# The values product of a fused two-block kernel: one fp32 product becomes three products of split operands

## The reference, cut to what matters

```python
sc = jnp.einsum('bqhd,bkhd->bhqk', q[:, s:e], k[:, :kend]).astype(jnp.float32) * scale
sc = jnp.where(mask[None, None], sc, -jnp.inf)
p = jax.nn.softmax(sc, axis=-1)
p = p.reshape(p.shape[0], A_HEADS, 2, e - s, kend)
w = p[:, :, 0] - lam * p[:, :, 1]
outs.append(jnp.einsum('bhqk,bkhd->bqhd', w.astype(v.dtype), v[:, :kend]))
```

## Time and profile before

| | us |
|---|---|
| median of 3 runs | 2394.51 (2392.45 to 2395.05) |
| the profiled execution, its own time | 2390.51 |
| its span in the trace | 2388.8 |
| PE busy | 2295.3 (96%) |
| PE weight loads busy | 1996.2 (84%) |
| DVE busy | 1601.9 (67%) |
| ACT busy | 1130.2 (47%) |
| POOL busy | 96.9 (4%) |

### The profile page before, as it was taken

One profiled execution on the slowest core, in us unless ns is written; L12 is line 12 of the kernel. 1 busy time (PEld: TensorE's weight loads), 2 busy tenths in 40 slices (PEclk: granted clock), 3 DMA queues, 4 the chain that ended last, 5 costly groups with the idle time before them and its releaser, 6 DMA issues.

```text
span 2388.8 us, 34521 instructions
## 1 busy us (share of the span) xinstructions
PE 2295.3 (96%) x13343; PEld 1996.2 (84%) x13343; DVE 1601.9 (67%) x1973; ACT 1130.2 (47%) x1693; POOL 96.9 (4%) x182
## 2 busy tenths in 40 slices
PE   6789999999989999999999999999999999999897
PEld 5678888887788888888888889999999999778786
DVE  6777677677768865666656776667667646666654
ACT  3345444443365543555445554444444455545443
POOL 0000000111100000000000000000000000000000
PEclk8789999999999999999999999999999999999999
DMA  9999788788857755555555655444444545433352
GB/s 337 357 358 357 255 265 280 232 314 311 317 176 252 271 198 187 183 190 179 194 194 176 210 179 164 157 142 142 142 142 142 167 151 153 146 124 107 106 194 106
DMA packets 229910, 492.95 MB, mean 206 GB/s; under 512 B 9618, under 2 KB 12392, under 8 KB 226696
## 3 DMA queue, kind: packets, MB, share of 16 engines
q1 hardware_dynamic: 210384, 432.05, 53.3%
q0 software_dynamic: 14144, 50.93, 6.4%
q10 hardware_dynamic: 5256, 8.20, 1.0%
HBM read 488.49 MB, written 2.10 MB: 205 GB/s over the span
## 4 chain that ended last, share of the span: by engine, by line
PE 82%; DVE 8%; DMA 4%; issue 2%; ACT 2%; SPq 0%; DVEq 0%; POOL 0%; POOLq 0%; ACTq 0%
PE ps L1722 31%; PE ps L1740 21%; PE ps L1755 14%; PE ps L1757 7%; DMA ada<-in_ada_w 2%; PE ps L2199 2%; DVE wlo L1029 2%; DVE acc L1089 2%; DMA mods<-in_ada_w 1%; PE ps L2026 1%; DMA raw<-in_a_w_in 1%; PE ps L2169 1%; ACT whi L521 1%; DVE acc L1038 1%; PE ps L1866 1%
## 5 line engine op out<-in xcount | busy, mean ns | idle before, releaser
L1029 DVE TENSOR_TENSOR wlo<-raw,whi 128x1024 fp32r<-128x1024 f32 x720 | 872.3, 1222 | 511.1 <-ACT whi L521 509.5
L521 ACT ACTIVATE whi<-raw 128x1024 fp32r<-128x1024 f32 x720 | 755.9, 1057 | 835.2 <-PE ps L1722 406.2
L1755 PE MATMUL ps<-xt__58,whi 128*128 128x512 f32 x1408 | 498.1, 399 | 0.9 <-DVE h L1221 0.7
L1757 PE MATMUL ps<-xt__58,wlo 128*128 128x256 f32 x1408 | 395.3, 281 | 0.0
L1722 PE MATMUL ps<-whi,xt__58 128*128 128x512 f32 x1024 | 331.9, 401 | 11.3 <-DVE xt__58 L1141 11.3
L1740 PE MATMUL ps<-xmh__59,whi 128*128 128x272 f32 x1088 | 323.3, 297 | 3.8 <-DVE ks L1426 3.1
L1755 PEld LDWEIGHTS ps<-xt__58,whi 128*128 128x128 f32 x1408 | 264.5, 188 | 67.3 <-DVE h L1221 2.2
L1740 PE MATMUL ps<-xmh__59,wlo 128*128 128x272 f32 x1088 | 315.7, 290 | 0.0
L1740 PE MATMUL ps<-xml__60,whi 128*128 128x272 f32 x1088 | 313.8, 288 | 0.0
L1757 PEld LDWEIGHTS ps<-xt__58,wlo 128*128 128x128 f32 x1408 | 266.0, 189 | 0.1
L1722 PEld LDWEIGHTS ps<-whi,xt__58 128*128 128x128 f32 x1024 | 196.9, 192 | 53.2 <-DVE xt__58 L1141 8.3
(11 more groups left out here) (297 smaller groups left out, 3272.6 us busy)
## 6 DMA issues: line engine op xcount, KB each, us to landing
raw<-in_a_w_in SPq DMA_DIRECT2D x128, 1024.0 KB, 5.3
raw<-in_ffn_w_up SPq DMA_DIRECT2D x88, 1024.0 KB, 5.1
ada<-in_ada_w POOLq DMA_DIRECT2D x96, 512.0 KB, 4.6
raw<-in_a_w_out SPq DMA_DIRECT2D x48, 1024.0 KB, 5.3
raw<-in_ffn_w_down SPq DMA_DIRECT2D x44, 1024.0 KB, 5.2
mods<-in_ada_w SPq DMA_DIRECT2D x64, 512.0 KB, 8.8
raw<-in_b_w_in SPq DMA_DIRECT2D x32, 1024.0 KB, 5.4
ada<-in_ada_w SPq DMA_DIRECT2D x16, 1024.0 KB, 12.2
```

The costliest lines, as they stand in the source:

```text
L521: act.activation(whi[:, r % 4], raw[:, r // 2, r % 2], ACT.Copy).then_inc(hi_ready, 1)
L1029: dve.tensor_tensor(wlo[:, r % 4], raw[:, r // 2, r % 2], whi[:, r % 4].bitcast(F32), ALU.subtract).then_inc(lo_ready, 1)
L1755: pe.matmul(both, whi[:, r % 4, i, c * P:c * P + P], xt_[:, :, k * T:k * T + T], start=first and i == 0, stop=last and i == 1, skip_group_ ...
L1757: mm = pe.matmul(ps[:, bank + c, 0:T], wlo[:, r % 4, i, c * P:c * P + P], xth[:, k, :], start=False, stop=last and i == 1, skip_group_chec ...
```

## The change: what it does, and the diff

The product of `wt` and the values is made as the projections are. `wt`, `vx0` and `vx1` get the type fp32r, so that ACT's copies round. DVE makes the rests: `wtl` from PSUM bank 6 and `wt`, at its step +7 of each item (one instruction per block), and `vl0` and `vl1` from banks 4 to 6 and the values' copies, in a new function `values_low` at its step 5 (six instructions per group). For each block PE does three products in place of one: `wt` by `vx`, `wt` by `vl`, `wtl` by `vx`. ACT now counts `a_wh` and `vx_high`; the semaphores `a_wt` and `vx_ready`, for which PE waits, are counted by DVE after the rests. So PE's transposes at step 2 and its scores at step 3 wait for DVE where they waited for ACT. Two pairs of semaphores of the first block are merged (`m2_spread` and `m5_spread` into `mod_spread`, `m2b_ready` and `m5b_ready` into `modb_ready`), with the counts adapted.

```diff
-        vx0 = place("vx0", [P, 3, 256], O_V + 3 * 4352)
-        vx1 = [place("vx1a", [P, 3, 256], O_V + 3 * 4352 + 3 * KB), place("vx1b", [P, 3, 256], O_ADA + 4352)]
+        vx0 = place("vx0", [P, 3, 256], O_V + 3 * 4352, F32R)
+        vx1 = [place("vx1a", [P, 3, 256], O_V + 3 * 4352 + 3 * KB, F32R), place("vx1b", [P, 3, 256], O_ADA + 4352, F32R)]
+        vl0 = place("vl0", [P, 3, 256], O_W + 17408 + 4352, F32R)
+        vl1 = [place("vl1a", [P, 3, 256], O_W + 17408 + 3 * 4352, F32R),
+               place("vl1b", [P, 3, 256], O_W + 17408 + 2 * 4352, F32R)]
...
-        wt = place("wt", [P, 3, P], O_V + 24640)
+        wt = place("wt", [P, 3, P], O_V + 24640, F32R)
+        wtl = place("wtl", [P, 3, P], O_ACC + 6528, F32R)
...
-                    cp.then_inc(sem("a_wt"), 1)
+                    cp.then_inc(sem("a_wh"), 1)
...
-                        cp.then_inc(sem("vx_ready"), 1)
+                        cp.then_inc(sem("vx_high"), 1)
...
+                for i, back in due(t, 7, items, before):
+                    dve.wait_ge(sem("a_wh"), (j - back) * 6 + (i + 1))
+                    for kb in ITEM_BLOCKS[i % 3]:
+                        w = BLK[kb][1]
+                        low = dve.tensor_tensor(wtl[0:w, kb, :], ps[0:w, 6, kb * P:kb * P + P], wt[0:w, kb, :].bitcast(F32),
+                                                ALU.subtract)
+                    low.then_inc(sem("a_wt"), 1)
+
+            def values_low(j):
+
+                for n, b in enumerate((2, 0, 1)):
+                    w, r = BLK[b][1], A_SCALE[b]
+                    dve.wait_ge(sem("vx_high"), j * 3 + (n - 2))
+                    for pair, (x, xl) in enumerate(((vx0, vl0), (vx1[j % 2], vl1[j % 2]))):
+                        low = dve.scalar_tensor_tensor(out=xl[0:w, b, :], in0=ps[0:w, 4 + b, pair * 256:pair * 256 + 256],
+                                                       scalar=st[0:w, r:r + 1], in1=x[0:w, b, :].bitcast(F32),
+                                                       op0=ALU.mult, op1=ALU.subtract)
+                    low.then_inc(sem("vx_ready"), 1)
...
                     if t == 0 and items:
                         rope(j - 1, 3)
+                    if t == 5 and items:
+                        values_low(j)
...
-                        mm = pe.matmul(ps[:, 7, 0:256], wt[0:w, kb, :], (vx1[(j - back + 1) % 2] if i > 2 else vx0)[0:w, kb, :],
-                                       start=kb == blocks[0], stop=kb == blocks[-1])
+                        p1 = (j - back + 1) % 2
+                        xh, xl = (vx1[p1], vl1[p1]) if i > 2 else (vx0, vl0)
+                        for m, (y, x) in enumerate(((wt, xh), (wt, xl), (wtl, xh))):
+                            mm = pe.matmul(ps[:, 7, 0:256], y[0:w, kb, :], x[0:w, kb, :],
+                                           start=kb == blocks[0] and m == 0, stop=kb == blocks[-1] and m == 2)
```

More of the change, by code:

```diff
@@ L656, in u_chunk @@
                             v_out(7, 1)
-                            act.wait_ge(sem("m2_spread"), 4)
+                            act.wait_ge(sem("mod_spread"), 4)
                             for n in range(4):
                                 act.activation(acc[:, 0, n * 512:n * 512 + 512], ps[:, 4 + n, :], ACT.Copy)\
-                                   .then_inc(sem("m2b_ready"), 1)
+                                   .then_inc(sem("modb_ready"), 1)
                         else:
@@ L809, in _ @@
                     if p == 0 and t == 10:
-                        act.wait_ge(sem("m5_spread"), 4)
+                        act.wait_ge(sem("mod_spread"), 8)
                         for n in range(4):
                             act.activation(acc[:, 0, n * 512:n * 512 + 512], ps[:, 4 + n, :], ACT.Copy)\
-                               .then_inc(sem("m5b_ready"), 1)
+                               .then_inc(sem("modb_ready"), 1)
                     cast(*at(gd, t))
@@ L1246, in _ @@
                         if n == 1:
-                            dve.wait_ge(sem("m2b_ready"), 4)
+                            dve.wait_ge(sem("modb_ready"), 4)
                         residual(n - 1, (n - 1) % 2, acc[:, 0], "resid", 0)
@@ L1376, in _ @@
                         if p == 0 and n == 1:
-                            dve.wait_ge(sem("m5b_ready"), 4)
+                            dve.wait_ge(sem("modb_ready"), 8)
                         residual(n - 1, (n - 1) % 2, acc[:, 0], "resid_f", 8 * p)
@@ L1527, in _ @@
                     rope(3, 3)
+                if t == 5:
+                    values_low(4)
                 if t % 8 == 3 and t > 8:
@@ L1881, in u_chunk @@
                     pe.wait_ge(mod_added, mod_adds(3, 7) + 16)
-                    row_all(0, "m2_spread")
+                    row_all(0, "mod_spread")
                 else:
@@ L1888, in u_chunk @@
                         if first:
-                            pe.wait_ge(sem("m2b_ready"), 4)
+                            pe.wait_ge(sem("modb_ready"), 4)
                         else:
@@ L1973, in pair @@
                     elif first and p == 1:
-                        pe.wait_ge(sem("m5b_ready"), 4)
+                        pe.wait_ge(sem("modb_ready"), 8)
                         pe.wait_ge(sem("vs_ready"), F)
@@ L1992, in _ @@
                         pe.wait_ge(ada_step, 96)
-                        row_all(1, "m5_spread")
+                        row_all(1, "mod_spread")
                     if n == 0 and r % 2 == 0:
```

## The result

The changed kernel takes 2401.13 us (median of 7 runs, 2398.57 to 2403.46); the kernel before takes 2394.51 (7 runs). The ratio is 1.0034 with a 95% interval of 1.0023 to 1.0044. A second measurement gave 1.0025 (1.0015 to 1.0035). So it is slower by a quarter to a third of a per cent, 6 to 8 us by the ratios; the medians themselves are 6.6 and 4.7 us apart. The time lies in the range of 2391 to 2403 us, near its upper end; the likeliest value, 2397.8, was 3.3 us too low.

A forecast was written before the change was run, and what follows sets the result against it. PE was taken to bound the kernel, with 82% of the chain. A saving of 2.6 us against losses of 4.0 (step 2) and 1.9 (copies of k) made 3.3 us slower, 2394.5 to 2397.8 us; range 2391.0 to 2403.0.

The forecast's parts named there:

- The product: PE's product of weights and values: three fp32r products at 0.357 us replace 0.43 per block, saving 0.073.
- the fixed 0.40 us: Cost per item on PE, seen as two idle gaps at the 16-row block's weight loads; forecast to stay.
- The wait at step 2: PE waits for DVE's values before item 5's transposes, three times, 1.35, 1.34 and 1.31 us; sum 4.0 us.
- The copies of k: Item 2's three rests delay DVE's copies of k, 0.63 us in each of groups 1 to 3; 1.9 us lost.
- Without a gap: Claim that DVE at steps 17 to 19, up to the copies of k, runs with no idle time.
- PE loses it one for one: At the copies of k, PE loses the rests' full 0.63 us (0.42 to 1.05) in groups 1 to 3.
- Covered waits: Rival: DVE has room at both waits, the saving counts in full, 3.5 us gained, 2391.0; chance 0.10.
- The fixed part goes: Rival: the fixed 0.40 us per item goes with fp32, 7.2 us more saved, 2390.6; chance 0.12.
- small loads in the open: Rival: two further 16-row loads each add a 0.20 us gap per item, 7.2 us more, 2405.0; chance 0.12.
- the upper quarter of the forecast: The forecast's part that is slower by more than 0.2%, counted as 0.14 of the 0.28 chance.
- the likeliest case: The forecast itself: both waits outweigh the product's saving, net 3.3 us slower (0.2 to 7.1), 2397.8; chance 0.64.

The follow-up runs named there:

- both2_pad: both2 with the 16-key block multiplied with 128 rows of weights, 112 of them zero; ratio 0.9942, 2378.06 us against 2393.79 for the kernel before.
- products_only: Changed kernel without DVE's rests, PE doing three products of the rounded operands per block; ratio 0.9991 to the kernel before, attention 412.2 us.
- both2: Changed kernel with copies of k ahead of item 3's scores, values' copies and rests one step earlier, rests behind item 4's normalised copy; attention 407.6 us.
- rests_only: Changed kernel with DVE's rests computed but unused, one fp32 product of the rounded operands per block; ratio 1.0041 to the kernel before, attention 424.6 us.
- merge_only: Kernel before with only the two pairs of semaphores of the first block merged; ratio 1.0005, attention 415.1 us.
- after_again: The changed kernel measured once more, no edit; ratio 1.0025 to the kernel before, attention 420.3 us.
- v_early: Changed kernel with the values' copies on ACT and their rests on DVE at step 4 in place of 5; attention 420.8 us.

## Why the prediction was right, and where its size was off

**The views.** The reading that PE counts, and that DVE's position at two places decides, was right. Both waits are in the trace after, three times each, and PE waits for DVE nowhere else in the attention. From the end of one wait at k to the next, a group lasts 89.0 us before and 90.1 after where no stretch at 1.2 GHz lies in it; 90.4 were predicted.

**The product.** An item was to take 1.47, 1.11 and 0.75 us for three, two and one block, and the trace shows 1605.68 - 1604.10 - 0.126 = 1.45, 1.10 and 1633.75 - 1632.75 - 0.252 = 0.75, the same way measured. That the fixed 0.40 us stays was right, and both2_pad shows why: it belongs to the change from 128 to 16 rows. The four passes that the Trainium skill gives for a true fp32 product (FP8 and Floating Point Precision, TensorE Precision Notes) promised an estimated 5.1 us; the old product's 0.43 us agrees with four passes of 0.107, but a pass of the new one costs 0.118, so that products_only, with items 2 and 4 swallowed three times each, gave 2.9, and both2 with all items but item 4 in three groups 3.4. These are the 0.073 us per block of the rows. The skill's statement that a change of tiling mode drains the engine (TensorEngine Tiling (Array Packing), Key Properties) fits what both2_pad shows, if 16 rows are another mode than 128, which no run here tells.

**The wait at step 2.** 1.35, 1.34 and 1.31 us were worked out, 1.2 measured. DVE's two rests took what was said (second one ending 0.88 us after the first's start). About half of the difference is the handing over, taken as 0.12 us from DVE's end to PE's load: here it is 1687.05 to 1687.10, 0.05. One reading was wrong: item 4's saving does not lengthen this wait. It is 1.2 us with the saving (after) and without it (rests_only), since the wait for ACT's copies of q has swallowed the saving before.

**The copies of k.** 0.63 us for three rests, 0.60 measured; the wait was to become 1.9 and is 1.9. "Without a gap" was not so: ahead of item 3's reciprocal DVE stands idle for 0.97 us, before and after, and waits for ACT's exponentials of scores that DVE itself has just made. The gap lies in the chain and gives no room, so the price came out right.

**The sum.** In the attention, free of stretches at the lower clock, 3.3 us were forecast. Measured: 420.4 - 2 x 1.55 = 417.3 against 415.1, 2.2 us. The losses were 3 x 1.22 + 3 x 0.60 = 5.5 us in place of 5.9, and the saving 2.9 (products_only, which loses the same items) in place of 2.6. That makes 2.6; the other 0.4 us belong to no single term.

**What was missing.** The step "PE loses it one for one" took the price of a wait to be its length. The sum has no term for what PE's clock does after one. The traces show 3.4 us at 1.2 GHz that begin at most 1.6 us behind the end of the wait at k (in rests_only just ahead of it), worth about 1.55 us (7.79 - 6.26, and 416.6 - 415.1), at 1 of 6 waits of 1.0 to 1.1 us (before, merge_only), at none of 3 of 1.3 (products_only), at all 3 of 1.6 (rests_only) and at 6 of 9 of 1.9 us (after, after_again, v_early). There was none in the attention of the six kernels where that wait is gone. So the longer wait made such stretches more frequent, in the traces of the changed kernel two to an execution in place of about one in two. The length isn't all of it, since the same 1.9 us brought one in two groups and none in the third. That is 1.5 x 1.55 = 2.3 us beside the 2.2, and 4.5 us in all, 2399.0. The forecast's own sum with this term would have been 2397.8 + 2.3 = 2400.1. The trace of before had shown one: its window 1683 to 1772 stood at 0.98 and its neighbours at 1.00; the prediction shows only the one from 1594 to 1683.

**The rivals.** "Covered waits" is refuted for this order of DVE's work and right for the one in both2. "The fixed part goes" and "small loads in the open" are both refuted by the product's times above. The outcome, slower by more than 0.2%, had a chance of 0.28. Half of that belonged to rivals that did not come about, and half to the upper quarter of the forecast, where the waits would have cost more than they do. It came about by the likeliest case with the clock on top. That the time still lies in the range is in part luck: the range was drawn wide for other reasons.

**What stays open.** 4.5 us against measured ratios of 1.0034 and 1.0025, that is 8.1 (5.5 to 10.5) and 6.0 (3.6 to 8.4) us. The second agrees with 4.5, the first only just doesn't. The stages outside the attention take 1972.2 to 1980.4 us in the thirteen traces, and merge_only shows no slowing from the semaphores. Whether a further 1 or 2 us are lost there isn't settled. How often the lower clock comes is counted in one trace to a run. The mean granted clock of all executions points the same way (0.981 before, 0.978 and 0.979 in the two measurements of the changed kernel, 0.978 in rests_only) but doesn't prove it: one stretch moves it by 0.0007 only, and products_only has 0.980 with no stretch in the attention of its trace. The lower clock was tied to the wait at k by moving the wait away, not by setting its length, and what else decides was not tried.

## What to carry to other kernels

When work is moved onto a second engine to relieve the first, look where in that engine's program the new instructions stand and who waits for what is behind them. Here PE's 3 us were lost in two places where what PE needs hung on DVE's work with no room, and three moves in the order of instructions (the copies of k, the values' copies, their rests) gave them back. A wait that is already there is the worst place to add to: it swallows the gain before it, grows one for one, and can bring a stretch at the lower clock. A saving counts only up to the next wait, for whichever engine. And look at the short blocks: a block of 16 rows among blocks of 128 cost 0.40 us per visit, more than the number format did, and rows of zeros removed it.

## What the runs showed of the hardware that was not expected

- A stretch of 3.4 us at 1.2 GHz after a wait of PE within a run that is busy at 99%: 7.79 us for 48 matmuls in place of 6.26. At the wait at k it came with 1 of 9 waits of 1.0 to 1.3 us and with 9 of 12 of 1.6 to 1.9 us, by PE's idle matmuls. With the 18 waits of 1.0 to 1.1 us at step 2, so measured, it never came.
- A product with 16 rows of weights behind another one costs 0.12 to 0.13 us (1619.13 to 1619.26), as one with 128 does, but each change between 16 and 128 rows costs 0.20, in fp32 and in fp32r. The 112 zero rows cost nothing that shows: 0.118 us per product.
